# A two-layer streaming encoder on one core: a later second turn at the borders between products, filler matmuls, an end that goes block by block, and nine tiles of a modulation unit multiplied as columns

## The reference

```python
cond = silu(c)
for layer in range(2):
    sh_m, sc_m, g_m, sh_f, sc_f, g_f = split(cond @ w_ada[layer] + b_ada[layer], 6)   # each 2048 long
    h = rms_norm(x, norm_mix_gain[layer]) * (1 + sc_m) + sh_m
    y = pool_mixer(h) if layer == 0 else hgrn2_mixer(h, hgrn_w_in, hgrn_w_out)
    x = x + g_m * y
    h = rms_norm(x, norm_ffn_gain[layer]) * (1 + sc_f) + sh_f
    a, b = split(h @ w_ffn_in[layer], 2)                                             # 2 x 5632 columns
    x = x + g_f * ((silu(a) * b) @ w_ffn_out[layer])
return rms_norm(x, final_gain)
```

## Time and profile before

| what | value |
|---|---|
| median of 3 runs | 2176.46 us (2176.29 to 2176.57) |
| the profiled execution | 2179.37 us, its span 2177.7 us |
| TensorE (PE) busy | 2130.3 us, 98% of the span |
| VectorE (DVE) busy | 1641.1 us, 75% |
| ScalarE (ACT) busy | 998.0 us, 46% |
| GpSimd (POOL) busy | 21.0 us, 1% |
| mean DMA rate | 264 GB/s |

### The profile page before, as it was taken

The page is one execution under the profiler, slowest core; times in us unless marked ns, Lnnn a source line. Parts: engine busy times, 40 slices in busy tenths (PEclk is TensorE's granted clock), DMA queues, the critical chain, the costliest instruction groups (busy, mean ns, idle before and its releaser), DMA issues.

```text
span 2177.7 us, 24635 instructions
## 1 busy us (share of the span) xinstructions
PE 2130.3 (98%) x9513; PEld 1724.8 (79%) x9513; DVE 1641.1 (75%) x1685; ACT 998.0 (46%) x1116; POOL 21.0 (1%) x89
## 2 busy tenths in 40 slices
PE   7999999999999999999999999999999999999997
PEld 3557887888888888878888888878888888888886
DVE  5779899999988887769787887677756666546644
ACT  2324544444444334455655566554454444444433
POOL 1000000000000000010000000000000000000000
PEclk9999999999999999999999999999999999999999
DMA  9998898988899998756666664578856556558664
GB/s 383 418 418 336 326 345 295 322 319 315 311 339 331 340 338 290 251 181 231 217 202 213 222 199 160 191 281 300 280 185 192 185 182 187 193 188 297 236 216 136
DMA packets 149105, 574.34 MB, mean 264 GB/s; under 512 B 16662, under 2 KB 16854, under 8 KB 141308
## 3 DMA queue, kind: packets, MB, share of 16 engines
q1 hardware_dynamic: 148988, 572.77, 74.6%
HBM read 570.60 MB, written 2.10 MB: 263 GB/s over the span
## 4 chain that ended last, share of the span: by engine, by line
PE 91%; DVE 4%; issue 2%; DMA 1%; ACT 1%; SPq 0%; DVEq 0%; ACTq 0%
PE prod L637 28%; PE prod L639 28%; PE prod L638 28%; DVE acc L1346 2%; PE modp L665 2%; PE small L708 1%; DMA ada<-in_ada_sections 1%; PE small L880 1%; PE modp L672 1%; DMA ada_head<-in_ada_sections 1%; PE modp L699 1%; PE small L855 0%; DVE part_value L1642 0%; PE small L901 0%; PE small L865 0%
## 5 line engine op out<-in xcount | busy, mean ns | idle before, releaser
L964 ACT ACTIVATE w_hi<-raw 128x1024 fp32r<-128x1024 f32 x696 | 736.0, 1061 | 988.9 <-PE prod L639 908.3
L1297 DVE TENSOR_TENSOR w_lo<-raw,w_hi 128x1024 fp32r<-128x1024 f32 x696 | 848.3, 1222 | 420.7 <-ACT w_hi L964 419.2
L637 PE MATMUL prod<-w_hi,h_hi 128*128 128x512 f32 x2072 | 818.9, 395 | 4.9 <-issue 1.9
L639 PE MATMUL prod<-w_hi,h_lo 128*128 128x512 f32 x2072 | 808.3, 390 | 0.0
L638 PE MATMUL prod<-w_lo,h_hi 128*128 128x512 f32 x2072 | 808.1, 390 | 0.0
L637 PEld LDWEIGHTS prod<-w_hi,h_hi 128*128 128x128 f32 x2072 | 390.1, 188 | 86.7 <-issue 3.1
L639 PEld LDWEIGHTS prod<-w_hi,h_lo 128*128 128x128 f32 x2072 | 389.9, 188 | 82.0
L638 PEld LDWEIGHTS prod<-w_lo,h_hi 128*128 128x128 f32 x2072 | 390.3, 188 | 79.0 <-issue 1.0
L1346 DVE SCALAR_TENSOR_TENSOR acc<-ada,cond,acc 128x1024 f32<-128x1024 f32 x255 | 326.1, 1279 | 0.4
L637 PE MATMUL prod<-w_hi,g_hi 128*128 128x512 f32 x688 | 268.8, 391 | 0.0
L639 PE MATMUL prod<-w_hi,g_lo 128*128 128x512 f32 x688 | 267.7, 389 | 0.0
(11 more groups left out here) (196 smaller groups left out, 1051.9 us busy)
## 6 DMA issues: line engine op xcount, KB each, us to landing
raw<-in_w_ffn_in SPq DMA_DIRECT2D x352, 512.0 KB, 4.6
ada<-in_ada_sections SPq DMA_DIRECT2D x256, 512.0 KB, 5.9
raw<-in_w_ffn_out SPq DMA_DIRECT2D x176, 512.0 KB, 4.3
raw<-in_hgrn_w_in SPq DMA_DIRECT2D x128, 512.0 KB, 3.6
ada_head<-in_ada_sections SPq DMA_DIRECT2D x36, 1024.0 KB, 15.7
raw<-in_hgrn_w_out SPq DMA_DIRECT2D x32, 512.0 KB, 3.5
ada<-in_ada_sections SPq DMA_DIRECT2D x12, 1024.0 KB, 12.0
ada<-in_ada_mixed SPq DMA_DIRECT2D x16, 512.0 KB, 7.3
```

Source lines behind the costliest of these rows:

```text
L637: pe.matmul(o, hi[:, k, ts], wh, start=(begin and s == 0), stop=False)
L639: mm = pe.matmul(o, lo[:, k, ts], wh, start=False, stop=(end and s == n - 1))
L964: act.activation(w_hi[:, slot], raw[:, r], ACT.Copy).then_inc(hi_ready, 1)
L1297: dve.tensor_tensor(w_lo[:, slot], raw[:, r], w_hi[:, slot], ALU.subtract).then_inc(lo_ready, 1)
```

## The change

It does seven things. (1) `multiply_columns`: the nine tiles of the head unit `MIX_F` that TensorE takes are no longer multiplied with the tile as the moving side and 512 columns, but as stationary blocks of 128 x 128 with `cond[:, k]` as one moving column, straight into the columns' sum; VectorE's row add for this unit goes. (2) `border_features`, `split_first`, `SECOND`: at a border only the first quarter is turned ahead of the product, the second turn stands at the product's step 2; the first quarter is normalised in two halves, each with its own signal; TensorE starts on `h_hi` of the first block and waits for `h_lo` only at its first use (`low_block`); the third pair of weights is split inside the border. (3) `stay_warm`: matmuls of the identity into a free `prod` buffer, whose result is overwritten, two of 512 columns behind the gate's reduction at H0 and A1, one of 256 behind the first turn, one of 512 and one of 256 at A0. (4) `BEHIND`: other first and last steps for the units, and the gates at H0 and A1 taken 12 steps later. (5) GpSimd's masks begin at step H0 + 14. (6) The last chunk of all does eight steps block by block instead of four, and all such steps wait for the low part pair by pair. (7) `last_blocks`: at the end each token block gets its own square, root, scaling and stores.

```diff
-    LAST, BLOCKED = (C_OUT0 + NCH - 1, C_WOUT + NCH - 1, C_OUT1 + NCH - 1), 4
+    SECOND, BORDER_AHEAD = 2, AHEAD + 2
+    BLOCKED = {C_OUT0 + NCH - 1: 4, C_WOUT + NCH - 1: 4, C_OUT1 + NCH - 1: 8}
...
-              ((0, SH_F, 1), A0 + 40, A0 + 72, None), ((0, SC_F, 1), A0 + 80, A0 + 108, A0 + 116),
+              ((0, SH_F, 1), A0 + 36, A0 + 62, None), ((0, SC_F, 1), A0 + 66, A0 + 108, A0 + 116),
...
-            multiplied(pool, C_H - 1)
+            pool.wait_ge(w_used, (H0 + 14) // 2)
...
             def last_steps(chunk, hi, lo, first):
-                g = t.get("step")
-                pe.wait_ge(lo_ready, (g + BLOCKED) // 2)
+                g, steps = t.get("step"), BLOCKED[chunk]
...
+                        if tb == 0 and s % 2 == 0:
+                            pe.wait_ge(lo_ready, (g + s) // 2 + 1)
...
+            def multiply_columns(u):
+                pe.wait_ge(unit_taken, u)
+                open_columns(u)
+                for k in range(folded(u)[0]):
+                    n = u * KD + k
+                    slot, _ = ada_slot(n)
+                    ada_arrived(pe, n)
+                    for j in range(UB):
+                        mm = pe.matmul(modp[:, 0, j:j + 1], ada_buffer(slot)[:, j * P:(j + 1) * P], cond[:, k:k + 1],
+                                       start=False, stop=False)
+                    mm.then_inc(ada_free[slot], 1)
...
+            def stay_warm(chunk, columns):
+                evacuated(pe, chunk - 2)
+                pe.matmul(prod[chunk % 2][:, 0, 0:columns], ident[:, :], fill_cols[:, 0:columns // P], start=True, stop=True)
...
-            multiply_loads(6)
+            multiply_columns(6)
             turn_normalised()
-            head_columns(6)
+            close_columns(6)
+            stay_warm(C_A0, CH)
+            stay_warm(C_A0, S)
...
             def features(k):
+                if k in (0, SECOND) or k and k % HG == 0 and k // HG + 1 < NCH:
+                    turn_normalised()
                 if k == 0:
-                    turn_normalised()
-                if k % HG == 0 and k // HG + 1 < NCH:
-                    turn_normalised()
+                    stay_warm(C_H, S)
                 wait_block(k)
...
             reduce_unit(BETWEEN[0])
+            for _ in range(2):
+                stay_warm(C_H, CH)
...
-                if in_columns(u) and k == last - 1:
+                if in_columns(u) and UNITS[u][1] != MIX_F and k == last - 1:
...
+            def border_features():
+                normalise(0)
+                lo()
+                split_first()
+                normalise(1, 1)
+                split_feat(0, 1)
...
-            act.activation(xs[:, 0, 0:D - CH], xs[:, 0, 0:D - CH], ACT.Copy, scale=rstd[:, 0:1]).then_inc(y_block, 1)
-            act.activation(xs[:, 1, 0:CH], xs[:, 1, 0:CH], ACT.Copy, scale=rstd[:, 1:2]).then_inc(y_block, 1)
+            def last_blocks():
...
+                for tb in range(TB):
...
+                    act.wait_ge(block_var, tb + 1)
+                    act.activation(rstd[:, tb:tb + 1], rstd[:, tb:tb + 1], ACT.Sqrt).then_inc(block_root, 1)
...
+                    scaled = xs[:, tb, 0:2 * CH if tb else D - CH]
+                    act.activation(scaled, scaled, ACT.Copy, scale=rstd[:, tb:tb + 1]).then_inc(y_block, 1)
```

More of the change, by code:

```diff
@@ L605, in last_steps @@
                     o = prod[chunk % 2][:, tb]
-                    for s in range(BLOCKED):
+                    for s in range(steps):
+                        if tb == 0 and s % 2 == 0:
+                            pe.wait_ge(lo_ready, (g + s) // 2 + 1)
                         k, slot = first + s, (g + s) // 2 % SPL
@@ L610, in last_steps @@
                         pe.matmul(o, hi[:, k, ts], wl, start=False, stop=False)
-                        mm = pe.matmul(o, lo[:, k, ts], wh, start=False, stop=(s == BLOCKED - 1))
-                        if tb == 0 and s == BLOCKED - 1:
+                        mm = pe.matmul(o, lo[:, k, ts], wh, start=False, stop=(s == steps - 1))
+                        if tb == 0 and s == steps - 1:
                             mm.then_inc(block_multiplied, 1)
@@ L615, in last_steps, with segment @@
                             mm.then_inc(w_used, 1)
-                t.tick("step", BLOCKED)
-            def segment(chunk, hi, lo, first, n, after=None, before=None, begin=True, end=True):
+                t.tick("step", steps)
+            def segment(chunk, hi, lo, first, n, after=None, before=None, begin=True, end=True, low=None):
                 par = chunk % 2
@@ L638, in segment @@
                         pe.matmul(o, hi[:, k, ts], wl, start=False, stop=False)
+                        if low is not None and s == 0 and tb == 0:
+                            low()
                         mm = pe.matmul(o, lo[:, k, ts], wh, start=False, stop=(end and s == n - 1))
@@ L647, in segment, with product, h_product @@
                             reduce_unit(u)
-            def product(hi, lo, first=0, after=None, before=None):
+            def product(hi, lo, first=0, after=None, before=None, low=None):
                 chunk = t.get("chunk")
-                segment(chunk, hi, lo, first, STEPS[chunk], after, before)
+                segment(chunk, hi, lo, first, STEPS[chunk], after, before, low=low)
                 t.tick("chunk")
-            def h_product(after=None, before=None, first=0):
-                product(h_hi, h_lo, first, after, before)
+            def h_product(after=None, before=None, first=0, low=None):
+                product(h_hi, h_lo, first, after, before, low)
             def multiply_loads(u):
@@ L700, in reduce_unit, with turn @@
                 mm.then_inc(unit_reduced, 1)
-            def turn(block_of):
+            def turn(block_of, ready=None):
                 for half in range(2):
                     bank(half)
+                    if ready is not None:
+                        pe.wait_ge(tok_ready, ready + half)
                     for j in range(2):
@@ L950, in _ @@
             reduce_unit(BETWEEN[1])
+            for _ in range(2):
+                stay_warm(C_A1, CH)
             ffn_in(1)
@@ L1737, in ffn_out @@
                     gains_of(C_GMIX + KD, 0, 0, KD, UNIT[(1, SC_M, 1)])
[L1738 removed]
+                if layer:
+                    last_blocks(base + NCH - 1, gate[:, 1], UNIT[(1, G_F, 1)])
+                    return
+                update_last(base + NCH - 1, NCH - 1, gate[:, 1], UNIT[(0, G_F, 1)])
                 last_root()
```

167 lines of the change are left out of this document (113 added, 54 removed).

## The result

The changed kernel takes 2183.64 us (2181.89 to 2183.85, 7 runs) against 2176.57 before (2176.14 to 2179.71, 7 runs): a ratio of 1.0025, 95% interval 1.0014 to 1.0036. It is slower by a quarter of a per cent. The profiled execution of the changed kernel took 2181.98, its span 2180.3. The forecast was 2162.7, with 2158 to 2177 as the range.

A forecast was written before the change was run, and what follows sets the result against it. PE holds 91% of the chain; gains were sought where it waits or runs at the low clock. Off the median 2176.46, −5.2 −2.0 −3.5 −0.1 −3.0 = −13.8 gave 2162.7 us, range 2158 to 2177.

The forecast's parts named there:

- A: End of the head: no row add, shorter sums and fillers start the product earlier and at full clock, −5.2 us.
- the price of the columns: End of the head: 144 one-column records at 0.122 us each, as where the clock was high, 17.6 us for all.
- the overlap: End of the head: columns end at 171.1 to 172.5, about when VectorE's last fold lets the sums start (172.45).
- the fillers ahead of the product: End of the head: with fillers, the product's first 14 records take 3.2 us instead of 6.05, another −2.85 us.
- B: Folds in A0: two and one in turn keep VectorE under PE's pace, so loader waits shrink, −2.0 us.
- The lost lead at the gate: A0: the fold behind the gate starts after its reduction, so VectorE waits and loses its lead, 0.5 to 1.0 us back.
- C: Border at H0: GpSimd moved, fillers, and one turn with its modulation and splits no longer ahead of the product, −3.5 us.
- the two terms in the product: Behind H0: first five matmuls at the high clock, −1.0 us; second turn inside the product at step 2, +0.9 to 1.06.
- the moved masks: After H0 + 14: GpSimd's masks could slow VectorE's splits by 0 to +3.5 us; 0 was taken.
- D: Border at A1: 1.6 us earlier, mostly given back by the turn within the product and a late `w_lo`, −0.1 us.
- E: Program end: a separate chain per token block, with block 0 ahead and a shorter last scaling, −3.0 us.
- Rival 1: End of the head: the columns don't keep the clock, product starts at 189 to 190, total 2178.3 us; chance 0.25.

The follow-up runs named there:

- E5: Changed kernel with 128 equal moving columns instead of one behind the nine tiles' loads, and the bias moved behind the tiles; 2167.48 us, ratio 0.9951.
- E1: Changed kernel with unit 6's nine tiles multiplied as rows of 512 columns again, with VectorE's row add; 2170.55 us, ratio 0.9964.
- E6: E1 without the head's two fillers ahead of A0; 2170.32 us.
- E7: E1 with two more 512-column fillers, in TensorE's waits for the row add and for the last fold; 2168.96 us, ratio 0.9956.
- E12: Changed kernel with 128 moving columns in nine tiles and their sums, bias behind the first tile, first fold behind A1 six steps later; 2165.75 us, ratio 0.9948.
- E10: E7 with the first and last steps of the units in A0 as in the kernel before; 2169.39 us.
- E3: The kernel before, unchanged, run again for a second trace; 2176.67 us.
- E9: E7 with GpSimd's masks started again when the last chunk before H0 is done; 2168.25 us.
- E8: E1 without the six fillers of the borders at H0 and A1; 2170.45 us.
- E2: The kernel before with one edit, unit 6 multiplied as columns; 2188.72 us, ratio 1.0052.
- E4: Changed kernel with one filler matmul of 512 columns behind each of the nine tiles' one-column matmuls; 2193.82 us, ratio 1.008.

## Why the prediction was wrong, step by step

**A (−5.2) failed, and with it the forecast.** The step that failed is the price of the columns, "so 0.122 each, or 17.6 us for all", and under it the overlap, by which they would be done at 171.1 to 172.5, about when VectorE's last fold lets the sums start. They took 27.5 and were done at 182.8, ten us late, since the clock fell during them. The forecast had the right row in hand, 24 one-column records at 0.50 with PE busy throughout, and named that the whole of A hung on it, but set it aside because that stretch "started low", and gave the case 0.25. The argument against it was a rule: that activity holds the clock, by which back-to-back columns would keep it. E5 beside the changed kernel shows what was wrong with it: the same blocks, loaded at the same rate, held the clock with 128 moving columns and lost it with one. The Trainium skill ("TensorE: Matmul & The Clock Gate", section "What's actually happening") speaks of how busy the engine is; in these traces an engine busy for 100% of a stretch by the profile had the low clock, and so busy time isn't what the rule can be read from. The same page's 107 ns a load (section "LDWEIGHTS (loading the stationary operand)") agrees with the traces at the high clock (0.114 in E5) and not at the low one (0.213 to 0.215).

The rest of A was half right. VectorE's row add does go. But the fillers ahead of the product don't give 2.85 us: they stand behind the sums, where the clock has already fallen (E1, E6). The gain exists, but in the waits ahead of the sums (E7's trace: 741.28 us from A0 to H0 instead of 743.43 in E6) or with no waits and wide columns (E12).

**B (−2.0)** has the right sign and mechanism; E10 measures −1.4. The term was too large because new waits, 1.3 to 1.5 us for `w_lo` and 0.3 to 0.6 for ScalarE's `part_value`, replace part of what goes. The lost lead at the gate was priced at 0.5 to 1.0.

**C (−3.5)** came out at −3.48 in this trace and −2.37 against E3, where the clock fell later in the border. The price was right for the execution and too large for the median. These are the border alone; the two terms in the product, −1.0 for a faster start and +1.0 for the second turn, cancel as forecast (the stretch is 493.08 before, 493.00 after), and it shows no cost of the moved masks either, the 0 that was chosen out of 0 to +3.5. The split of the gain into GpSimd and clock was partly wrong: GpSimd is 0.7 of it (E9), the fillers nothing (E8), the rest is the shorter chain and the clock that no longer falls. What holds the clock stays open: E9 has GpSimd in the border but also the fillers, E8 has neither, and no run has GpSimd there without fillers.

**D (−0.1)**: the border gained 1.64 and the product lost 1.85, so +0.2. The mechanisms behind the loss are the two given, the turn within the product and VectorE late for `w_lo`, with 0.77 us of wait. But I had the wrong culprit: at 1444.20 and 1445.06 two folds stand ahead of the two splits that end the wait. Moving the first fold by six steps (E12) gave 1.0 us back.

**E (−3.0)** measured −3.06.

**Rival 1's time, 2178.3,** was 5 us too low although its product start (189 to 190) was right. Against E3, whose execution is at the median of before, its head was taken as +10.5 instead of +12.3 and its other gains as 8.6 instead of 6.9. The remaining 1.7 is the spread of the changed kernel's own executions (its trace is at 2181.98, its median at 2183.64). The range ended at 2177 because the rival's chance was too small and its time too low; with the sum made against a trace 2.9 us above the median, the whole forecast was biased by about that much.

## What to carry to other kernels

A matmul with one moving column is not cheap work: price a long run of them at the low clock, and look at the granted clock of the nearest such run in the trace, whatever the busy time says. If the stationary loads set the pace anyway, spread the moving column until it fills the time of the load; here 128 equal columns cost nothing and gave back 16 us. Put fillers in front of the first small work behind dense work, in the waits themselves, not behind it (in the trace that gained 2.5 us at the product's start, but not in every execution); and before a gain is taken off a median, ask whether the profiled execution had the same losses as the median one.

## What the runs showed of the hardware

With PE and its loader 100% busy on one-column float32 matmuls, the granted clock went from 1.00 to 0.50 (0.78 as the mean of the first 7 us in the changed kernel; one tile at full pace in E2 and E4, about two in the changed kernel, by its 64 records in 10.53 us) and stayed there for over 20 us. Eight one-column matmuls and one of 512 columns in turn stayed at 0.50 too (E4). With 128 moving columns behind the same loads it stayed at 1.00 for 16 us (E5, E12). Sixteen one-column records of sums with no idle stretch ahead ended at 0.50 behind one such stream (E5), and with two fillers among what stood ahead of them at 1.00 (E7, the execution traced). Sixteen records with one moving column and sixteen with 128 take the same 1.95 us at the high clock (E7, E12). A `normalise` of 256 columns was 1.5 times as long beside GpSimd's mask building (E9), a two-input split of 1024 columns 1.02 times.
